# One more weight unit split ahead of the second and of the third norm's chain in a two-layer encoder trunk

## The reference, cut to what matters

```python
for layer in range(DEPTH):                                     # 2 layers, 256 tokens, D_MODEL 1024
    ada = c_act @ ada_w[layer] + ada_b[layer]
    sh1, sc1, gt1, sh2, sc2, gt2 = jnp.split(ada, 6, axis=-1)
    h = modulate(rmsnorm(x, norm_mix_w[layer]), sh1, sc1)      # norms 0 and 2
    x = x + gt1[:, None, :] * token_mixer(h, ...)              # projections, delta rule, attention
    h = modulate(rmsnorm(x, norm_ffn_w[layer]), sh2, sc2)      # norms 1 and 3
    f = swiglu(h, ...) if layer % 2 == 0 else moe_swiglu(h, ...)
    x = x + gt2[:, None, :] * f
return rmsnorm(x, final_norm_w)
```

## Time and profile before

| | |
|---|---|
| time, median of 3 runs | 1778.49 us (1778.14 to 1779.12) |
| time of the profiled execution | 1779.29 us |
| its span, first to last instruction | 1777.5 us |
| busy share of the span | PE 98%, DVE 82%, ACT 61% |
| mean granted clock of PE | 0.994 of full speed |
| second norm, last block of the mixer to first matmul of the rising unit | 277.3 to 281.45 us |
| third norm, the same | 534.3 to 539.46 us |
| expert stage | from about 786 us to the end |

### The profile page before, as it was taken

The page is one execution under the profiler, slowest core; times in us unless marked ns, Lnnn a source line. Parts: engine busy times, 40 slices in busy tenths (PEclk is TensorE's granted clock), DMA queues, the critical chain, the costliest instruction groups (busy, mean ns, idle before and its releaser), DMA issues.

```text
span 1777.5 us, 26736 instructions
## 1 busy us (share of the span) xinstructions
PE 1735.5 (98%) x10287; PEld 1511.2 (85%) x10290; DVE 1464.0 (82%) x1420; ACT 1085.7 (61%) x953; POOL 73.1 (4%) x131
## 2 busy tenths in 40 slices
PE   6999999999999999999999999999999999999997
PEld 6989999999998899987788888888888888888875
DVE  6877678878858664679988898988889888989898
ACT  4564355333335644567677777777777777777775
POOL 4010000000000100000000000010000000000000
PEclk8999999999999999999999999999999999999999
DMA  9744566988973333469999999999999999999994
GB/s 311 246 157 147 162 205 218 337 311 298 330 245 119 119 90 101 142 218 360 337 370 385 360 375 367 363 386 369 357 389 359 371 387 360 374 368 364 389 391 161
DMA packets 261447, 519.97 MB, mean 293 GB/s; under 512 B 12170, under 2 KB 75892, under 8 KB 261364
## 3 DMA queue, kind: packets, MB, share of 16 engines
q1 hardware_dynamic: 257988, 506.21, 80.4%
q0 software_dynamic: 3376, 12.58, 1.8%
HBM read 510.90 MB, written 7.86 MB: 292 GB/s over the span
## 4 chain that ended last, share of the span: by engine, by line
PE 87%; DVE 8%; ACT 2%; issue 2%; DMA 1%; POOL 0%; DVEq 0%; SPq 0%; ACTq 0%; POOLq 0%
PE bank L1124 17%; PE bank L1126 17%; PE bank L1125 17%; PE bank L1130 9%; PE bank L1131 8%; PE bank L1132 8%; DVE w_lo L1965 2%; DVE w_lo L1801 2%; PE bank L1728 1%; PE bank L1424 1%; PE bank L1461 1%; PE bank L1145 1%; DVE ada_acc L1819 1%; ACT w_hi L1046 1%; DMA ring<-in_ada_w_dram 1%
## 5 line engine op out<-in xcount | busy, mean ns | idle before, releaser
L1965 DVE TENSOR_TENSOR w_lo<-ring,w_hi 128x2048 fp32r<-128x2048 f32 x336 | 767.1, 2290 | 94.7 <-ACT w_hi L1046 90.0
L1046 ACT CAST w_hi<-ring 128x2048 fp32r<-128x2048 f32 x336 | 642.2, 1912 | 137.2 <-PE bank L1126 131.1
L1124 PE MATMUL bank<-w_hi,xg_hi 128*128 128x512 f32 x896 | 357.3, 399 | 0.8 <-DVE w_lo L1965 0.7
L1126 PE MATMUL bank<-w_hi,xg_lo 128*128 128x512 f32 x896 | 353.4, 394 | 0.0
L1125 PE MATMUL bank<-w_lo,xg_hi 128*128 128x512 f32 x896 | 353.0, 394 | 0.0
L1130 PE MATMUL bank<-hT_hi,w_hi 128*128 128x256 f32 x1040 | 300.5, 289 | 6.3 <-DVE w_lo L1801 4.9
L1131 PE MATMUL bank<-hT_lo,w_hi 128*128 128x256 f32 x1040 | 293.7, 282 | 0.0
L1132 PE MATMUL bank<-hT_hi,w_lo 128*128 128x256 f32 x1040 | 293.5, 282 | 0.0
L1801 DVE TENSOR_TENSOR w_lo<-ring,w_hi 128x2048 fp32r<-128x2048 f32 x94 | 214.6, 2290 | 65.8 <-ACT w_hi L759 65.8
L759 ACT CAST w_hi<-ring 128x2048 fp32r<-128x2048 f32 x94 | 178.9, 1906 | 59.7 <-PE bank L1132 56.3
L1130 PEld LDWEIGHTS bank<-hT_hi,w_hi 128*128 128x128 f32 x1040 | 198.5, 191 | 10.5 <-DVE w_lo L1801 4.8
(11 more groups left out here) (434 smaller groups left out, 2014.3 us busy)
## 6 DMA issues: line engine op xcount, KB each, us to landing
ring<-in_moe_w_gate_dram SPq DMA_DIRECT2D x112, 1024.0 KB, 7.1
ring<-in_moe_w_up_dram SPq DMA_DIRECT2D x112, 1024.0 KB, 7.2
ring<-in_moe_w_down_dram SPq DMA_DIRECT2D x112, 1024.0 KB, 7.2
ring<-in_ada_w_dram SPq DMA_DIRECT2D x48, 1024.0 KB, 6.9
ring<-in_w_in_dram SPq DMA_DIRECT2D x38, 1024.0 KB, 5.6
ring<-in_ffn_w_gate_dram SPq DMA_DIRECT2D x14, 1024.0 KB, 7.3
ring<-in_ffn_w_up_dram SPq DMA_DIRECT2D x14, 1024.0 KB, 6.8
ring<-in_ffn_w_down_dram SPq DMA_DIRECT2D x14, 1024.0 KB, 6.8
```

The costliest lines, as they stand in the source:

```text
L1046: act.copy(w_hi[MOE_BUF[p % NS_MOE]][:], ring[:, p % RING, :]).then_inc(hi_ready, 1)
L1124: pe.matmul(o, xh, wh, start=start, stop=False)
L1126: return pe.matmul(o, xl, wh, start=False, stop=stop)
L1965: dve.tensor_tensor(w_lo[b][:], ring[:, p % RING, :], f32(w_hi[b][:]), ALU.subtract).then_inc(taken, 1)
```

## The change

Two splits move ahead, and the buffers of the second mixer are swapped so that one of them can. At the second norm ACT casts `("fu",0)` before it begins the squares, and DVE takes its rest behind the last add of `add_blocks`, before the scaling. At the third norm both engines split `("qkvz",1,1)` before the chain: ACT before the squares, DVE before the first add. In layer 1's mixer `b = s % 2` becomes `(s + 1) % 2`, and `MOE_BUF` follows so that the expert stage meets the same buffers free.

```diff
         elif k == ("mix", L - 1, 1, 1):
             b, last_in[2] = 2, split_keys.index(("wa", L - 1, 1))
         else:
-            b = s % NS_MIX
+            b = (s + k[1]) % NS_MIX
         buf_of.append(b)
...
-    MOE_BUF = (1, 0, 2)
+    MOE_BUF = (0, 1, 2)
...
                 ahead(("mix", l, 1, 1), 1)
                 if l == 0:
+                    ahead(("fu", 0), 0)
                     act.preload_act_table_set("natural_log_exp_and_others")
                     squares_x(1, f_sq, f_tmp)
...
                         f_high(i)
-                    ahead(("qkvz", 1, 0), 0)
+                    ahead(("qkvz", 1, 1), 0)
                     act.preload_act_table_set("natural_log_exp_and_others")
...
                     norm_scale(1)
                     ahead(("fg", 0), 0)
                     add_blocks(1, 2, f_sq)
+                    ahead(("fu", 0), 0)
...
                     ahead(("fd", 2 * FC - 1), 0)
-                    ahead(("qkvz", 1, 0), 0)
+                    ahead(("qkvz", 1, 1), 0)
                     add_blocks(2, 5, f_sq)
```

## The result

| | before | changed |
|---|---|---|
| median of 10 executions each | 1778.43 us | 1783.7 us |
| lowest, highest | 1777.73, 1779.71 | 1780.54, 1784.95 |
| profiled execution, its span | 1779.29, 1777.5 us | 1783.75, 1782.0 us |

The ratio is 1.0024, with a 95% interval from 1.0016 to 1.0031: slower. The middle of the interval lies over the 0.2% that can be told from no change, its lower end does not. The changed kernel's times stand in two groups, three at 1780.5 to 1781.5 us and seven at 1783.2 to 1785.0 us; the profiled execution is one of the seven.

What follows compares the result with a forecast made beforehand. PE was taken to bound the kernel (busy 98% of the span). Nets of 0.3 and 1.0 us at the norms plus 1.1 for the clock gave +2.4 us, 1780.9 us against the median of 1778.49; range 1778.8 to 1782.8.

Steps and rivals of the forecast that it cites:

- The nets of 0.3 and 1.0 us: Second and third norm: chain 1.7 and 2.5 us late, less removed waits of 1.36 and 1.43 us.
- a sum of 1.3: Both norms' nets together, 0.3 + 1.0 us, by the instructions and without any loss of clock.
- the term of 1.1 us: Third norm: PE's clock falls after 3.6 us idle, costing 1.1 us.
- its bound of 1.7 us for one fall: Third norm: a clock fall costs at most 1.7 us, if all of it is on the chain.
- the expert stage's row: 774.5 to 780 us: mean granted clock 0.69, taken as 1.7 us of full-speed work lost, one fall's price.
- the slower rival: Clock low through the sums into the rising unit, or at both norms: +4.7 us, 1783.2; chance 13%.
- the nearer of its two figures: Total by the cited clock rule +2.4 us or more; by the norms' own rows, clock at 1.00, +1.3.
- a short fall: Forecast case: delays as worked out and one short clock fall at the third norm; 1779.9 to 1782.0 us, chance 53%.
- the clock did not stay full: Rival at the norms: the clock stays full, +1.3 us, 1779.8; chance 22%.
- the splits were not free: Rival at both norms: early splits cost the chain nothing, both waits go, -2.8 us, 1775.7; chance 9%.
- nothing was gained elsewhere: Rival: faster by over 0.2%, needing free splits and 0.8 us from elsewhere, such as the mixer's later rests; chance 3%.

Runs made afterwards that it cites:

- the change with filling: The whole change plus 16 matmuls with unused results on PE, between the last down block and the third norm's sums of squares; ratio 1.0007.
- The delay alone: Kernel before, buffers and splits kept; at the third norm DVE waits, then forms one rest twice before its first add; 1.0025, +4.9 us by medians.
- e6_bias_first: The whole change with the router bias's eight products moved ahead of the third norm's sums of squares; 1.0013, +1.5 us by the medians.

## Why the prediction was right or wrong

**The place of the loss and its mechanism: right.** Both norms' chains were delayed by the early splits, and every time that the prediction names for the instructions came within 0.3 us, with the 1.25 or 0.98 us added: first square 275.05 us (275.0), last add 279.43 (279.4), scaling 282.22 (282.0), first add of the third norm 533.22 (533.2), sixth 536.71 (536.7), gap before the sums 3.64 us (3.6). Both waits behind the rising units are gone. The nets of 0.3 and 1.0 us measured 0.27 in the change's profile and 0.81 in that of the change with filling, together 1.1 against a sum of 1.3; by that run's medians it is 0.9, by its ratio 1.2.

**The clock: the event right, the size wrong.** The step that failed is the term of 1.1 us, "a fall at the third norm, with the chain's matmuls hit and part of it in the small ones that nobody waits for", and its bound of 1.7 us for one fall, read from the expert stage's row. It measured 4.6 us in the profiled execution: 5.6 us late at the next unit's end, less 2.5 for the chain's delay, plus the 1.43 of the wait removed; against the filled version it is 4.8. The clock was at 1.2 GHz from about 537.5 to 547.5 us. Of the loss, 1.1 us is in the sums (2.70 against 1.58). Some 1.8 us is in the small products and the constant matmuls behind them, which the prediction took for work that nobody waits for: at 3.42 us in place of 1.85 the products end behind the arrival of the first scaled block, which in the kernel before came just as PE was through with them (the rising unit starts at 539.46 us, 0.65 us behind the start of ACT's first block at 538.81; that is the distance at which PE followed a block that it waited for at the second norm, 281.45 against 280.80). The run with these products moved shows it. The other 1.8 us is the rising unit's own matmuls, 7.8 us from its start to its end against 5.9.

The price was also read from the wrong row. The 1.7 us are those of one short fall in the expert stage, where PE never stood still. The same trace of the kernel before has a fall of some 14 us at 27 to 41 us, with 3.18 us of idleness in it and small matmuls around. The prediction does not use it, and by it a bound of 1.7 us for one fall had no ground.

**The price of a fall and the gain are not independent.** My sum added them. The delay alone shows that when the clock falls for long, the wait behind the rising unit vanishes by itself, so the fall costs 3.1 us to a kernel that still has this wait (5.89 - 2.83) and 4.8 to one that has not (5.57 - 0.81). For the change it makes the whole gain of 1.4 us void at the third norm.

**The total.** Forecast 1780.9 us, median 1783.7 us, above the high end of 1782.8. The ratio of 1.0024 is +4.3 us, the medians are 5.3 apart, about what the slower rival gave (+4.7, 1783.2): clock low through the sums and into the rising unit. It got 13%; the profiled execution is such a one, and seven of ten have its time. The three others, at 1780.5 to 1781.5 us, are where the forecast stood; no profile shows whether for the forecast's reason, a short fall. The other rivals are out for the profiled execution: the clock did not stay full, the splits were not free, and nothing was gained elsewhere.

**The rule that the prediction cites.** The Trainium skill (TensorE: Matmul & The Clock Gate, Part 1) expects PE's clock to fall to half behind an idle stretch and to stay there until PE has been busy again for a while. The trace agrees: 3.64 us without an instruction, then 0.58 and 0.50 of the clock until some 10 us later, while PE ran the sums, the small products and the first half of the rising unit. By this rule the prediction had +2.4 us or more, the nearer of its two figures.

**Not settled:** why the clock stays down for some 10, 7 or 4 us, or perhaps not at all, in executions of nearly the same instructions; the profiles show one execution each. And where the filled version's slower executions lose what the two forms of the start do not explain, some 2 of their 3.5 us.

## What to carry to other kernels

An operation moved ahead "into an idle stretch" must be placed against what the engine is waited for next, on each engine by itself: the same 2.2 us of DVE work cost 2.5 us ahead of the first add of a chain, and hardly anything behind the last, where DVE waits for others anyway. A table load behind an early cast was part of the delay; in front of it, it cost nothing. A gap that grows on PE is more than its length: look for every fall of the clock that the trace has, not only the nearest or the shortest, take the price from all that stands between the gap and the next full unit, the small products too, and keep PE busy with something or move such products into the gap. Gains and losses in a row of waits do not add: a wait that was removed is worth nothing in executions in which its partner has become slower. And to compare two executions, measure from one instruction to another around the change, not from the start of the span: what the clock did elsewhere is in the total.

## What the runs showed that was not expected

One idle stretch of 3.6 us on PE was followed by some 10 us at 1.2 GHz (0.58, 0.50, 0.50 and 0.63 granted from 537 to 548 us), a stretch where the kernel before had its full clock. In the one fall that the earlier trace rows show of the kernel before, in the expert stage, it was 0.69 on the mean of 5.5 us; the long fall at its start had 0.73 from 25 to 30 us and 0.50 from there to 40. Gaps of 1.65 us at the second norm (five profiles) and 1.82 us at the third (one) were followed by none. But a gap of 1.96 us directly behind eight-column matmuls was, with 0.60 granted from 537 to 540 us (`e6_bias_first`).

The mean clock of a whole execution is no measure of one stretch. The profiled executions of the kernel before and of the change both have 0.994, one with its long fall at the start, the other at the third norm.
